# Reordering the last two experts of a one-core attention and mixture-of-experts layer: up, up, down, down, with the last down weights in smaller pieces and the output sent from two queues

## The chip, the cores and the metric

The kernel runs on one core of a Trainium2 chip. The metric is the device time of that core in microseconds (us). All matrices are fp32.

## What is computed

One layer over 256 tokens of 1024 features: an attention part with two kinds of heads, then a mixture of 32 experts, of which each token uses 4, and a final normalisation. The part that matters here, cut from the reference:

```
def clamped_swiglu(h):
    g = jnp.minimum(h[..., 0::2], SWIGLU_LIMIT)
    u = jnp.clip(h[..., 1::2], -SWIGLU_LIMIT, SWIGLU_LIMIT)
    return g * jax.nn.sigmoid(SWIGLU_ALPHA * g) * (u + 1.0)

def expert_block(args):                      # for every expert, on the tokens routed to it
    xb, e = args
    a = clamped_swiglu(xb @ w_up[e] + b_up[e])     # w_up[e]   1024 x 2048
    return a @ w_down[e] + b_down[e]               # w_down[e] 1024 x 1024
...
x = x + moe_ffn(...)                         # sum of the experts' rows times their router weights
return rmsnorm(x, final_norm_g)              # over the 1024 features
```

All 32 experts are computed, so all 32 pairs of weight matrices (12.6 MB each) pass from HBM to the core.

## The kernel before

**Weights.** An expert's weights are six units of 2 MB: four of `w_up` (u = 0 to 3) and two of `w_down` (u = 4 and 5). They pass through a ring of ten units in SBUF (`ring`), filled by DMAs that SyncE (SP) issues in order. Units are counted by g = 6 b + u, where b is the expert. A unit g is loaded once unit g-10 has been used (`used(g - UNITS)`; semaphores `up_used` and `down_used`). For the last expert, b = 31, unit u = 3 and unit u = 5 are loaded as two halves each (`load_half`, line 482), and the second half has a semaphore of its own, `last_half_in`.

**TensorE (PE).** The engine's instructions stand in the order in which the code writes them. For an expert b (`run`): `up_bias` (line 1109), `up` (line 1129: 16 fp32 matmul records for each unit), `gather(b+1)` (line 1084: tokens of the next expert), `combine(b-1)` (line 1174: adds the previous expert's rows times router weights to the four output banks 4 to 7), `combine_turn(b)` (line 1142), `gather_turn(b+1)` (line 1099), `act_turn(b)` (line 1148: transposes the activations), `down` (line 1162: 16 records for each unit). The result of `down` lies in PSUM bank `XG`.

**VectorE (DVE) and ScalarE (ACT).** `swiglu` (lines 1613, 1614, 1616, 1620) and ACT's `sigmoid` (line 811) turn the up product into activations. `act_turn` waits for them (`a_ready`). After it DVE (line 1648) and ACT (line 820) each copy half of the transposed activations `aT` to SBUF, which `down` waits for. ACT copies the combine weights `cT` (line 818) and, after `down`, its result `yv` (line 823), which `combine` waits for.

**The last expert before.** Its order on PE is `up`, `combine(30)`, `combine_turn(31)`, `act_turn(31)`, `down`, `combine(31)`. Its swiglu is written in two halves (`swiglu_last`, lines 1626 to 1644, and ACT lines 850 and 852): the first half starts when the first half of the up product's columns is complete (`half_up`).

**The end.** Each of the four output banks is squared and summed by ACT (`square_sum`, line 874) as `combine(31)` completes it. DVE adds the two sums of a token tile (`mean`, line 1349), ACT takes the root (`take_root`, line 663), and DVE inverts it (`invert`, line 1354). Tile 0 is scaled by DVE (line 1758) and ACT (line 888), tile 1 by DVE (`finish`, line 1762). SP issues the four output DMAs of 256 KB (lines 579 and 581).

Of the kernel before, what the change touches and what calls it, by code (L numbers as in the profile page):

```python
# [20 lines left out]
P = 128  # L21
# [13 lines left out]
EPS = 1e-5  # L35


def hybrid_layer(nc, x, attn_norm_g, w_in, cmp_pe_k, cmp_pe_v, cmp_w1_k, cmp_w2_k, cmp_w1_v, cmp_w2_v, w_out,
# [53 lines left out]
    with ctx:  # L92
# [118 lines left out]
        aT = xg.rearrange("p (a b) -> p a b", a=4)  # L211
        xgT = carve(512, 8, 64)
        dump = [xg, xgT.rearrange("p a b -> p (a b)")]
        cnt = carve(1)
# [41 lines left out]
        last_half_in = {u: sem(f"last_half_in{u}") for u in (3, 5)}  # L256
# [76 lines left out]
        half_up = sem("half_up")  # L333
        last_swi = sem("last_swi")
        last_sig = sem("last_sig")
# [9 lines left out]
        half_summed = sem("half_summed")  # L345
        scaled_by_g = sem("scaled_by_g")
# [47 lines left out]
        def job_bank(name):  # L394
            return ps[:, PJ[job_at[name] % 2], :]

# [36 lines left out]
        def _(sp):  # L433
# [126 lines left out]
            for g in range(EXPERT_UNITS * LATE, EXPERT_UNITS * E):  # L560
                b, u = g // EXPERT_UNITS, g % EXPERT_UNITS
# [90 lines left out]
        def _(act):  # L652
# [159 lines left out]

            def read_rest(b, prev):

                act.wait_ge(cT_done, b + 1)
                if prev:
                    act.wait_ge(comb_done, b)
                act.activation(cT, ps[:, XG, 0:256].rearrange("p (n q) -> p n q", n=2), ACT.Copy).then_inc(cT_read, 1)  # L818
                act.wait_ge(aT_done, b + 1)
                act.activation(aT[:, 0:2, :], UP[:, 0, 0:256].rearrange("p (a q) -> p a q", a=2), ACT.Copy)\  # L820
                   .then_inc(aT_read, 1)
                act.wait_ge(down_used, b * DOWN_UNITS + DOWN_UNITS)
                act.activation(yv, ps[:, XG, :], ACT.Copy).then_inc(y_read, 1)  # L823
# [53 lines left out]
            flat = work[:, 0:3 * 512].rearrange("p (a b) -> p a b", a=3)  # L877
            square_sum(0, 0, flat[:, 0, :])
            square_sum(0, 1, flat[:, 1, :])
            square_sum(1, 0, flat[:, 2, :])  # L880
            take_root(4)
            square_sum(1, 1, dump[1])
            take_root(5)
            act.wait_ge(rstd_ready, 5)
            for half in range(2):
                h = slice(512 * half, 512 * half + 512)
                act.wait_ge(scaled_by_g, half + 1)
                act.activation(xs[:, 0, h], xs[:, 0, h], ACT.Copy, scale=rstd[:, 4:5]).then_inc(fin_act, 1)


        @block.tensor
        def _(pe):
# [221 lines left out]
            def up(b, prev, unit, biased=False, last=False, halves=False):  # L1114
# [4 lines left out]
                for u in range(UP_UNITS):  # L1119
                    w = unit(u)  # L1120
                    for j in range(2):
                        k = 2 * u + j
                        if last and k == KD - 1:
                            pe.wait_ge(last_half_in[u], 16)
                        row = aside if halves and k == 1 else w[:, j * 2 * F:(j + 1) * 2 * F]
                        row = row.rearrange("k (p h x) -> k p h x", h=2, x=8)
                        for a in range(2):
# [4 lines left out]
                            if last and k == KD - 1 and a == 0:  # L1132
                                t.then_inc(half_up, 1)
# [4 lines left out]
            def combine_turn(b, ahead):  # L1138
                pe.wait_ge(pw_ready, b + 1)
                pe.wait_ge(xg_read, b + 1 + ahead)  # L1140
                for n in range(NT):
                    t = pe.transpose(ps[:, XG, n * P:(n + 1) * P], pw[:, n, :], ident[:, :])  # L1142
# [9 lines left out]
            def down(b, unit, last=False):  # L1152
# [3 lines left out]
                for u in range(DOWN_UNITS):  # L1156
                    w = unit(UP_UNITS + u)
                    for j in range(4):
                        if last and (u, j) == (1, 2):
                            pe.wait_ge(last_half_in[UP_UNITS + u], 16)  # L1160
                        for h in range(2):
                            t = pe.matmul(ps[h * 64:(h + 1) * 64, XG, :],  # L1162
                                          aT[:, j, u * 64:u * 64 + 64],
                                          w[:, j * D + h * 512:j * D + (h + 1) * 512],
                                          start=(u == 0 and j == 0), stop=(u == DOWN_UNITS - 1 and j == 3),
                                          skip_group_check=True)
                    t.then_inc(down_used, 1)

            def combine(b, first=False, last=False):

                pe.wait_ge(y_read, b + 1)
                for n in range(NT):
                    for h in range(2):
                        t = pe.matmul(ps[:, OUT[n][h], :], cT[h * 64:(h + 1) * 64, n, :], yv[h * 64:(h + 1) * 64, :],  # L1174
                                      start=first, stop=True, skip_group_check=True)
                        if last and (n, h) != (1, 1):
                            t.then_inc(half_summed, 1)
                t.then_inc(comb_done, 1)

# [8 lines left out]
            def in_singles(b):  # L1188

                def unit(u):  # L1190
                    pe.wait_ge(*single_in(EXPERT_UNITS * b + u))
                    return single(EXPERT_UNITS * b + u)
# [106 lines left out]
            for b in range(TAIL, E - 1):  # L1299
# [31 lines left out]
        def _(dve):  # L1331
# [290 lines left out]
            def swiglu_last(b):  # L1622

                lo, hi = slice(0, 64), slice(64, P)
                dve.wait_ge(half_up, 1)
                dve.tensor_scalar(t1[:, :, lo], up_pairs[:, 0][:, :, lo], 7.0, None, ALU.min).then_inc(last_swi, 1)
                dve.tensor_scalar(t3[:, :, lo], up_pairs[:, 1][:, :, lo], 7.0, -7.0, ALU.min, ALU.max)\
                   .then_inc(last_swi, 1)
                dve.wait_ge(last_swi, 2)
                dve.scalar_tensor_tensor(out=t3[:, :, lo], in0=t3[:, :, lo], scalar=1.0, in1=t1[:, :, lo],  # L1630
                                         op0=ALU.add, op1=ALU.mult).then_inc(last_swi, 1)
                dve.wait_ge(up_used, b * UP_UNITS + UP_UNITS)
                dve.tensor_scalar(t1[:, :, hi], up_pairs[:, 0][:, :, hi], 7.0, None, ALU.min).then_inc(swi, 1)
                dve.tensor_scalar(t3[:, :, hi], up_pairs[:, 1][:, :, hi], 7.0, -7.0, ALU.min, ALU.max).then_inc(swi, 1)
# [163 lines left out]
```

## Time and profile before

| what | value |
|---|---|
| runs of the kernel | 1081.4, 1081.66, 1081.82 us, median 1081.66 us |
| span of the profiled execution, first to last instruction | 1078.8 us |
| whole device time of the profiled execution | not given by itself; the median of the runs lies 2.9 us above the span |
| PE busy | 1028.3 us, 95% |
| mean transfer rate from HBM | 392 GB/s over the span |
| granted TensorE clock | 0.999 of full speed |

The span is what the rows below are measured in. The 2.9 us around it lie outside of every row.

### The profile page before, as it was taken

To read this page: it belongs to the slowest core of one execution; us is meant where nothing else is said; L and a number is where in the kernel's file an instruction comes from. 1 tells how busy PE (TensorE), PEld (TensorE's weight loads), DVE (VectorE), ACT (ScalarE), POOL (GpSimd) and SP (SyncE) were. 2 spreads that over 40 slices of the span, in tenths; PEclk is the share of its full clock that TensorE was granted. 3 is DMA by queue.
4 is the path that set the end of the run, shared out by engine and by line. 5 is a ranking of instruction groups with operands and counts; after the bars stand their busy time and mean duration, and the time that the engine had idled before them with its cause. 6 is when DMAs were issued, how large, how long until landed. Compare 5 with 4: busy or idle time off the path is not lost.

```text
span 1078.8 us, 12673 instructions
## 1 busy us (share of the span) xinstructions
PE 1028.3 (95%) x5097; PEld 409.9 (38%) x5097; DVE 223.3 (21%) x637; ACT 155.0 (14%) x388; POOL 20.6 (2%) x49
## 2 busy tenths in 40 slices
PE   7899999999999999999999999999999999999996
PEld 5686654333333333333333333333333333333332
DVE  3344433111111111111111111111112101111112
ACT  2323332011000011111111111111101100111102
POOL 4001000000000000000000000000000000000000
PEclk9999999999999999999999999999999999999999
DMA  9982469999999999999999999999999999999994
GB/s 281 315 313 93 157 252 378 399 405 426 429 426 433 433 431 430 432 431 432 430 433 429 435 431 433 431 429 435 431 431 431 430 433 424 428 427 427 428 426 201
DMA packets 36827, 423.34 MB, mean 392 GB/s; under 512 B 8226, under 2 KB 12370, under 8 KB 18996
## 3 DMA queue, kind: packets, MB, share of 16 engines
q1 hardware_dynamic: 36644, 422.37, 93.8%
q8 instruction: 31, 0.51, 0.2%
q10 hardware_dynamic: 144, 0.39, 0.1%
q14 instruction: 8, 0.07, 0.0%
HBM read 421.70 MB, written 1.05 MB: 392 GB/s over the span
## 4 chain that ended last, share of the span: by engine, by line
PE 77%; DMA 18%; DVE 3%; ACT 1%; issue 1%; DVEq 0%; SPq 0%
PE ps L1129 31%; DMA ring<-in_w_up_dram 18%; PE ps L1162 17%; PE ps L1174 5%; PE ps L1084 4%; PE ps L916 4%; PE ps L994 3%; PE ps L923 2%; PE ps L1109 2%; PE ps L945 1%; DVE work L1604 1%; PE ps L1099 1%; DVE work L1648 1%; PE ps L1142 1%; PE ps L1021 1%; PE ps L1033 1%
## 5 line engine op out<-in xcount | busy, mean ns | idle before, releaser
L1129 PE MATMUL ps<-ring,work 128*64 128x512 f32 x2040 | 447.2, 594 | 8.3 <-DMA ring<-in_w_up_dram 8.2
L1129 PEld LDWEIGHTS ps<-ring,work 128*64 128x64 f32 x2040 | 142.8, 137 | 309.7 <-issue 290.9
L1162 PE MATMUL ps<-ring,work 128*64 128x512 f32 x1008 | 223.3, 595 | 21.1 <-DVE work L1648 21.1
L1613 DVE TENSOR_SCALAR work<-ps 128x512 f32<-128x512 f32 x31 | 21.4, 691 | 641.4 <-PE ps L1129 641.4
L1162 PEld LDWEIGHTS ps<-ring,work 128*64 128x64 f32 x1008 | 69.8, 137 | 154.4 <-issue 129.0
L811 ACT ACTIVATE work<-work 128x512 f32<-128x512 f32 x31 | 19.5, 630 | 453.1 <-DVE work L1613 453.1
L1174 PE MATMUL ps<-work 64*128 64x512 f32 x256 | 63.6, 615 | 0.7 <-ACT work L823 0.7
L1084 PE MATMUL ps<-xt,work 128*64 128x512 f32 x256 | 60.6, 593 | 0.2 <-DVE work L1562 0.2
L823 ACT ACTIVATE work<-ps 128x512 f32<-128x512 f32 x32 | 19.1, 597 | 236.6 <-PE ps L1162 236.6
L916 PE MATMUL ps<-ring 128*128 128x256 f32 x192 | 42.5, 380 | 0.0
L916 PEld LDWEIGHTS ps<-ring 128*128 128x128 f32 x192 | 36.0, 190 | 5.0 <-issue 0.4
L1174 PEld LDWEIGHTS ps<-work 64*128 64x128 f32 x256 | 22.0, 186 | 41.8 <-issue 40.2
L1109 PE MATMUL ps<-work 32*64 32x512 f32 x256 | 34.8, 613 | 0.5 <-ACT work L846 0.5
L1604 DVE TENSOR_TENSOR work<-ps,gf_rowsT 128x512 f32<-128x512 f32 x32 | 22.1, 692 | 54.3 <-PE ps L1099 54.3
L1084 PEld LDWEIGHTS ps<-xt,work 128*64 128x64 f32 x256 | 18.2, 137 | 35.8 <-issue 35.4
L994 PE MATMUL ps<-ring,extra 128*128 128x512 f32 (+1 forms) x72 | 28.7, 546 | 0.0
L923 PE MATMUL ps<-ring 128*128 128x280 f32 (+1 forms) x64 | 21.9, 497 | 0.0
L1616 DVE SCALAR_TENSOR_TENSOR work<-work 128x512 f32<-128x512 f32 x31 | 21.5, 692 | 1.1
L1620 DVE TENSOR_TENSOR work<-work 128x512 f32<-128x512 f32 x31 | 21.4, 692 | 1.1
L1614 DVE TENSOR_SCALAR work<-ps 128x512 f32<-128x512 f32 x31 | 21.1, 680 | 0.0
L805 ACT ACTIVATE work<-ps 128x512 f32<-128x512 f32 x32 | 19.1, 597 | 11.2 <-PE ps L1084 11.2
L818 ACT ACTIVATE work<-ps 128x256 f32<-128x256 f32 x32 | 12.3, 385 | 51.0 <-PE ps L1142 51.0
(245 smaller groups left out, 521.3 us busy)
## 6 DMA issues: line engine op xcount, KB each, us to landing
ring<-in_w_up_dram SPq DMA_DIRECT2D x40, 4096.0 KB, 35.1
ring<-in_w_up_dram SPq DMA_DIRECT2D x44, 2048.0 KB, 16.6
ring<-in_w_down_dram SPq DMA_DIRECT2D x20, 4096.0 KB, 35.0
ring<-in_w_down_dram SPq DMA_DIRECT2D x21, 2048.0 KB, 14.8
ring<-in_w_in_dram SPq DMA_DIRECT2D x8, 1024.0 KB, 8.5
ring<-in_w_up_dram SPq DMA_DIRECT2D x7, 1024.0 KB, 12.0
ring<-in_w_out_dram SPq DMA_DIRECT2D x4, 1024.0 KB, 10.0
ring<-in_w_down_dram SPq DMA_DIRECT2D x4, 1024.0 KB, 29.1
```

The costliest lines, as they stand in the source:

```text
L916: t = pe.matmul(dst, lhs(win_unit(c, k)), xT[:, k, :], start=(k == 0), stop=(k == KD - 1))
L923: t = pe.matmul(dst, xT[:, k, n * P:(n + 1) * P], win_unit(c, k)[:, lo:hi], start=(k == 0), stop=(k == KD - 1))
L994: t = pe.matmul(dst, oT[:, k, n * P:(n + 1) * P], wout_nsa[:, k, lo:hi] if k < 4 else wout_moba[:, lo // 512, k % 4, lo % 512:lo % 512 + h ...
L1084: t = pe.matmul(ps[h * 64:(h + 1) * 64, XG, :], pm[:, n, :], xt[:, n, h * 512:(h + 1) * 512], start=(n == 0), stop=(n == 1), skip_group_ch ...
L1109: t = pe.matmul(UP[h * 64:h * 64 + 64, a, :], sel[a * E:a * E + E], bup[a * E:a * E + E, :].rearrange("e (p h x) -> e p h x", h=2, x=8)[:, ...
L1129: t = pe.matmul(UP[h * 64:h * 64 + 64, a, :], xgT[:, k, :], row[:, a * 64:(a + 1) * 64, h, :], start=False, stop=(k == KD - 1), skip_group ...
L1162: t = pe.matmul(ps[h * 64:(h + 1) * 64, XG, :], aT[:, j, u * 64:u * 64 + 64], w[:, j * D + h * 512:j * D + (h + 1) * 512], start=(u == 0 a ...
L1174: t = pe.matmul(ps[:, OUT[n][h], :], cT[h * 64:(h + 1) * 64, n, :], yv[h * 64:(h + 1) * 64, :], start=first, stop=True, skip_group_check=True)
L1604: dve.tensor_tensor(xgT.rearrange("p (h j) t -> p j h t", h=2), ps[:, XTB, :].rearrange("p (j h t) -> p j h t", j=4, h=2), gf_rowsT[:].uns ...
L1613: dve.tensor_scalar(t1, up_pairs[:, 0], 7.0, None, ALU.min).then_inc(swi, 1)
L1616: dve.scalar_tensor_tensor(out=t3, in0=t3, scalar=1.0, in1=t1, op0=ALU.add, op1=ALU.mult)\
L1620: dve.tensor_tensor(av, t3, t2, ALU.mult).then_inc(a_ready, 1)
```

## The change

The order of the last two experts becomes up(30), up(31), down(30), down(31), both in the loads (`turn_of` and `unit_of`) and on PE. The rows of down(31) go to PSUM bank `XTB`, and the transposed activations and combine weights of expert 31 to `aT_end` and `cT_end` (the places of `t1` and `t2`). `combine(30)` stands between the two units of down(31). Unit u = 3 of expert 31 is loaded in one piece, and its swiglu is the ordinary one. Unit u = 5 of expert 31 is loaded as one half and two quarters, with a semaphore each (`last_row_in`). In the final normalisation ACT takes the root from its own second sum, with the first sum (already divided and with the epsilon added, `end_base`) as the bias. ACT issues the output DMAs of tile 0 itself. The diff, cut to its core:

```diff
+        aT_end = t1
+        cT_end = t2[:, 0:2, :]
...
+        def turn_of(b, u):
+
+            if b < E - 2:
+                return EXPERT_UNITS * b + u
+            if u < UP_UNITS:
+                return EXPERT_UNITS * (E - 2) + UP_UNITS * (b - (E - 2)) + u
+            return EXPERT_UNITS * (E - 2) + 2 * UP_UNITS + DOWN_UNITS * (b - (E - 2)) + u - UP_UNITS
+
+        unit_of = {turn_of(b, u): (b, u) for b in range(E) for u in range(EXPERT_UNITS)}
...
-                b, u = g // EXPERT_UNITS, g % EXPERT_UNITS
+                b, u = unit_of[g]
                 used(g - UNITS)
-                if b == E - 1 and u in last_half_in:
+                if (b, u) == (E - 1, EXPERT_UNITS - 1):
                     load_half(b, u, 0, half_of(single(g), 0), place_in[spot(g - 1)])
-                    load_half(b, u, 1, half_of(single(g), 1), last_half_in[u])
+                    for i in range(2):
+                        sp.dma_start(single(g)[:, (2 + i) * D:(3 + i) * D], down_v[b][:, (6 + i) * D:(7 + i) * D])\
+                          .then_inc(last_row_in[i], 16)
...
-                sp.wait_ge(fin_act, half + 1)
-                sp.dma_start(out_v[0][:, h], xs[:, 0, h]).then_inc(out_sent, 16)
                 sp.wait_ge(fin_dve, half + 1)
                 sp.dma_start(out_v[1][:, h], xs[:, 1, h]).then_inc(out_sent, 16)
...
-            with act.Fori(TAIL, E - 1) as i:
+            with act.Fori(TAIL, E - 2) as i:
                 run(i)
-            act.wait_ge(last_swi, 1)
-            act.activation(t2[:, :, 0:64], t1[:, :, 0:64], ACT.Sigmoid, scale=1.702).then_inc(last_sig, 1)
-            act.wait_ge(swi, (E - 1) * 3 + 1)
-            act.activation(t2[:, :, 64:P], t1[:, :, 64:P], ACT.Sigmoid, scale=1.702).then_inc(sig_done, 1)
+            select(E - 1, E - 1)
+            sigmoid(E - 2)
+            read_xg(E - 1)
+            act.wait_ge(comb_done, E - 2)
+            read_cT(E - 2, cT, XG)
+            read_aT(E - 2, aT)
+            sigmoid(E - 1)
             act.activation(root[:, 5:6], ident[:, 0:1], ACT.Sqrt)
-            read_rest(E - 1, True)
+            read_aT(E - 1, aT_end)
+            read_cT(E - 1, cT_end, XTB)
+            read_y(E - 2)
+            act.wait_ge(down_used, E * DOWN_UNITS)
+            act.wait_ge(comb_done, E - 1)
+            act.activation(yv, ps[:, XTB, :], ACT.Copy).then_inc(y_read, 1)
...
+            def end_root(n):
+                act.wait_ge(squared[0], 8 + 2 * n)
+                act.wait_ge(base_ready, n + 1)
+                act.activation(root[:, 4 + n:5 + n], sq_sum[:, 4 + n, 1:2], ACT.Sqrt, scale=1.0 / D, bias=ms[:, 4 + n:5 + n])\
+                   .then_inc(rooted, 1)
...
                 act.activation(xs[:, 0, h], xs[:, 0, h], ACT.Copy, scale=rstd[:, 4:5]).then_inc(fin_act, 1)
+                act.wait_ge(fin_act, half + 1)
+                act.dma_start(out_v[0][:, h], xs[:, 0, h]).then_inc(out_sent, 16)
...
-            last = in_singles(E - 1)
-            up(E - 1, True, last, last=True)
+            unit, last = in_singles(E - 2), in_singles(E - 1)
+            up(E - 2, True, unit)
+            gather(E - 1)
+            combine(E - 3)
+            combine_turn(E - 2, 1)
+            gather_turn(E - 1)
+            act_turn(E - 2)
+            up(E - 1, True, last)
+            act_turn(E - 1)
+            combine_turn(E - 1, 0, XTB)
+            down(E - 2, unit)
+            pe.wait_ge(aT_read, E * 2)
+            pe.wait_ge(cT_read, E)
+            down_unit(E - 1, 0, last(UP_UNITS), aT_end, XTB)
             combine(E - 2)
-            combine_turn(E - 1, 0)
-            act_turn(E - 1)
-            down(E - 1, last, last=True)
-            combine(E - 1, last=True)
+            down_unit(E - 1, 1, last(UP_UNITS + 1), aT_end, XTB, last=True)
+            combine_end(E - 1)
...
-            swiglu_last(E - 1)
-            read_aT(E - 1)
+            swiglu(E - 1)
+            read_aT(E - 1, aT_end)
...
             dve.wait_ge(gfin_in, 16)
+            end_base(0)
             scale_by_g(0)
-            mean(4, ((0, 8),))
             scale_by_g(1)
+            end_base(1)
             invert(4)
-            mean(5, ((0, 10),))
             invert(5)
```

`down_unit` is the body of the old `down` for one unit, with the place of the activations and the bank as arguments; with `last=True` it waits for `last_row_in` before each of its two last quarters. `combine_end` is `combine` with `cT_end`, and counts each output bank as the old last `combine` did.

## Rows read from the trace of the kernel before

**Rows 1.** Stretch 1040 to 1060 us, by windows: busy per engine, clock, DMA share, GB/s.

```profile
1040.00:1060.00 20.00, 19.68 (x95) 6.00 (x92) 2.66 (x8) 2.14 (x4) 0.00 (x0) 1.00 1.00 421
```

**Rows 2.** PE's waits over the span: total us, times, longest.

```profile
PE ps L1129 <- DMA ring<-in_w_up_dram: 8.2, 9, 1.4
```

**Rows 3.** Timeline of PE, 1026 to 1072 us: start, us, instructions, idle before.

```profile
1026.35 3.65 PE L1129 MATMUL ps<-ring,work 128*64 128x512 f32 x16 [1.24 <-DMA ring<-in_w_up_dram]
...
1033.85 0.60 PE L1099 MATMUL ps<-ident,work 128*128 128x128 f32 x4
1034.28 0.60 PE L1148 MATMUL ps<-ident,work 128*128 128x128 f32 x4
...
1035.56 7.09 PE L1162 MATMUL ps<-ring,work 128*64 128x512 f32 x32 [0.68 <-DVE work L1648]
...
1042.58 1.09 PE L1109 MATMUL ps<-work 32*64 32x512 f32 x8
...
1043.60 7.09 PE L1129 MATMUL ps<-ring,work 128*64 128x512 f32 x32
...
1051.00 7.09 PE L1129 MATMUL ps<-ring,work 128*64 128x512 f32 x32 [0.32 <-DMA ring<-in_w_up_dram]
...
1058.02 1.99 PE L1174 MATMUL ps<-work 64*128 64x512 f32 x8
...
1060.34 0.66 PE L1148 MATMUL ps<-ident,work 128*128 128x128 f32 x4
...
1061.51 7.09 PE L1162 MATMUL ps<-ring,work 128*64 128x512 f32 x32 [0.52 <-DVE work L1648]
...
1069.30 1.99 PE L1174 MATMUL ps<-work 64*128 64x512 f32 x8 [0.70 <-ACT work L823]
```

**Rows 4.** Timeline of DVE, swiglu and aT copy of expert 30.

```profile
1030.05 0.69 DVE L1613 TENSOR_SCALAR work<-ps 128x512 f32<-128x512 f32 x1 [23.06 <-PE ps L1129]
...
1032.10 0.69 DVE L1620 TENSOR_TENSOR work<-work 128x512 f32<-128x512 f32 x1
...
1035.09 0.41 DVE L1648 COPY work<-ps 128x256 f32<-128x256 f32 x1
```

**Rows 5.** Last weight loads: PE's wait for the tenth, then two issues with landings.

```profile
1055.97 0.37 PEld L1129 LDWEIGHTS ps<-ring,work 128*64 128x64 f32 x4 [0.48 <-DMA ring<-in_w_up_dram]
...
L472 SPq DMA_DIRECT2D ring<-in_w_down_dram x1: 4357/4357/4357, 1017.7 to 1017.7; - x1
DMA to landing us min/median/max: 43.1/43.1/43.1
...
L482 SPq DMA_DIRECT2D ring<-in_w_down_dram x2: 4240/4241/4242, 1022.1 to 1026.4; - x2
DMA to landing us min/median/max: 39.4/40.3/41.2
```

**Rows 6.** The end of the timeline, and ACT's two early DMA issues.

```profile
1073.16 0.15 DVE L1349 TENSOR_REDUCE ms<-sq_sum 128x1 f32<-128x2 f32 x1 [0.48 <-ACT work L874]
1073.35 0.29 ACT L663 ACTIVATE root<-ms,eps 128x1 f32<-128x1 f32 x1 [0.29 <-DVE ms L1349]
...
1073.88 1.41 DVE L1762 SCALAR_TENSOR_TENSOR extra<-ps,rstd,extra 128x512 f32<-128x512 f32 x2
...
1075.66 0.45 SPq L581 DMA_DIRECT2D out_dram<-extra  x1
...
L749 ACTq DMA_DIRECT2D work<-in_b_up_dram x2: 389/414/439, 80.3 to 80.7; - x2
```

**Rows 7.** PE's first instruction, and clock and DMA of two stretches.

```profile
6.90 1.94 PE L898 MATMUL ps<-ident,extra 128*128 128x128 f32 x8 [6.90 <-ACT extra L669]
...
3.00:6.00 3.00, 0.00 (x0) 0.00 (x0) 1.79 (x9) 1.22 (x4) 2.76 (x4) 1.00 1.01 338
...
1075.50:1076.00 0.50, 0.00 (x0) 0.00 (x0) 0.00 (x0) 0.00 (x0) 0.00 (x0) 0.74 1.01 373
```

More of the change, by code:

```diff
@@ L255, in hybrid_layer @@
         pair_in = [sem(f"pair_in{u}") for u in range(PAIRS)]
-        last_half_in = {u: sem(f"last_half_in{u}") for u in (3, 5)}
+        last_row_in = [sem(f"last_row_in{i}") for i in range(2)]
         prm_in = sem("prm_in")
@@ L345, in hybrid_layer @@
         half_summed = sem("half_summed")
+        base_ready = sem("base_ready")
         scaled_by_g = sem("scaled_by_g")
@@ L1112, in up_bias, with up @@
                 t.then_inc(bias_used, 1)
-            def up(b, prev, unit, biased=False, last=False, halves=False):
+            def up(b, prev, unit, biased=False, halves=False):
                 if not biased:
@@ L1122, in up @@
                         k = 2 * u + j
-                        if last and k == KD - 1:
-                            pe.wait_ge(last_half_in[u], 16)
                         row = aside if halves and k == 1 else w[:, j * 2 * F:(j + 1) * 2 * F]
@@ L1136, in up, with combine_turn @@
                     t.then_inc(up_used, 1)
-            def combine_turn(b, ahead):
+            def combine_turn(b, ahead, bank=XG):
                 pe.wait_ge(pw_ready, b + 1)
@@ L1150, in act_turn, with down_unit, down @@
                 t.then_inc(aT_done, 1)
-            def down(b, unit, last=False):
+            def down_unit(b, u, w, acts, bank, last=False):
+                for j in range(4):
+                    if last and j >= 2:
+                        pe.wait_ge(last_row_in[j - 2], 16)
+                    for h in range(2):
+                        t = pe.matmul(ps[h * 64:(h + 1) * 64, bank, :],
+                                      acts[:, j, u * 64:u * 64 + 64],
+                                      w[:, j * D + h * 512:j * D + (h + 1) * 512],
+                                      start=(u == 0 and j == 0), stop=(u == DOWN_UNITS - 1 and j == 3),
+                                      skip_group_check=True)
+                t.then_inc(down_used, 1)
+            def down(b, unit):
                 pe.wait_ge(aT_read, b * 2 + 2)
@@ L1156, in down, with combine @@
                 for u in range(DOWN_UNITS):
[L1157 to L1169, printed above, removed]
+                    down_unit(b, u, unit(UP_UNITS + u), aT, XG)
+            def combine(b, first=False, weights=cT):
                 pe.wait_ge(y_read, b + 1)
@@ L1173, in combine, with combine_end @@
                     for h in range(2):
-                        t = pe.matmul(ps[:, OUT[n][h], :], cT[h * 64:(h + 1) * 64, n, :], yv[h * 64:(h + 1) * 64, :],
+                        t = pe.matmul(ps[:, OUT[n][h], :], weights[h * 64:(h + 1) * 64, n, :], yv[h * 64:(h + 1) * 64, :],
                                       start=first, stop=True, skip_group_check=True)
-                        if last and (n, h) != (1, 1):
-                            t.then_inc(half_summed, 1)
                 t.then_inc(comb_done, 1)
+            def combine_end(b):
+                pe.wait_ge(y_read, b + 1)
+                for n in range(NT):
+                    for h in range(2):
+                        pe.matmul(ps[:, OUT[n][h], :], cT_end[h * 64:(h + 1) * 64, n, :], yv[h * 64:(h + 1) * 64, :],
+                                  start=False, stop=True, skip_group_check=True)\
+                          .then_inc(half_summed if (n, h) != (1, 1) else comb_done, 1)
             def in_pairs(m, c):
@@ L1190, in unit @@
                 def unit(u):
-                    pe.wait_ge(*single_in(EXPERT_UNITS * b + u))
-                    return single(EXPERT_UNITS * b + u)
+                    pe.wait_ge(*single_in(turn_of(b, u)))
+                    return single(turn_of(b, u))
                 return unit
@@ L1298, in _ @@
                     run(m * CYCLE + (SINGLES + r), in_pairs(m, r))
-            for b in range(TAIL, E - 1):
+            for b in range(TAIL, E - 2):
                 table_read = tables(b)
@@ L1753, in total, with end_base @@
                 return ps[:, OUT[n][half], :]
+            def end_base(n):
+                dve.wait_ge(squared[0], 7 + 2 * n)
+                dve.tensor_scalar(ms[:, 4 + n:5 + n], sq_sum[:, 4 + n, 0:1], 1.0 / D, EPS, ALU.mult, ALU.add)\
+                   .then_inc(base_ready, 1)
             def scale_by_g(half):
```

67 lines of the change are left out of this document (23 added, 44 removed).

## The prediction

> **What bounds the kernel now.** I read four views, from the whole to the end. The windows come first: between 1040 and 1060 us PE is busy 19.68 of 20 us and the DMA engines are full at 421 GB/s [rows 1]. So in the expert stage both resources are nearly exhausted together. Second, the waits: PE waited for weights only nine times, 8.2 us in all [rows 2]. The stream of weights is the slower of the two, by a little. Third, PE's timeline over the last two experts [rows 3] with the landings of the last loads [rows 5]. The reader is to see where the stream stops deciding. Call the last twelve units of the stream the 1st to the 12th. The 9th lets PE go on at 1051.00 [rows 3], the second half of the 10th at 1055.97, the 11th lands at 1017.7 + 43.1 = 1060.8, and the two halves of the 12th at 1022.1 + 41.2 = 1063.3 and 1026.4 + 39.4 = 1065.8 [rows 5]. That is 4.9 us for a unit, while PE needs 3.44 us for one (7.09 for x32 less 3.65 for x16 [rows 3]). From 1051 on PE never waits for weights again except for that half: down(31) runs without a break from 1061.51 to 1068.60 [rows 3], and its last quarter, due at some 1067.7, had landed 2 us before. Fourth, the end of the timeline [rows 6]: after 1068.60 comes a chain of copies, sums, root, scaling and output.
>
> So the question is not when the last weights land but what PE still has to do, and what it waits for, from the point where the new order departs from the old.
>
> **The new order step by step.** The first new instruction on PE stands after `act_turn(30)`, where `down(30)` used to start at 1035.56, released by DVE's copy of `aT` (1035.09 + 0.41 [rows 4]). `up_bias(31)` waits for the same copy, so it starts at 1035.56 too. No load is gated differently: the last twelve loads wait for units of experts 28 and 29 and the first two of expert 30, whose use does not move, and all units are equally large. I therefore keep the landings by place in the stream.
>
> - Bias: 1042.58 to 1043.60, thus 1.02 us [rows 3]; up(31) starts at 1036.58.
> - up(31): 3.65 + 3 x 3.44 = 13.97 us, to 1050.55. Its units are now the 5th to 8th; the 8th lands about 4.9 us before the 9th, near 1046.1, and is wanted at 1036.58 + 3 x 3.44 = 1046.9. No wait for weights.
> - swiglu(31) lies bare. `act_turn(31)` is next on PE and waits for it, and queued behind it are `combine_turn(31)` and all of `down(30)`, whose activations have been ready since 1035.5. The ordinary swiglu takes 0.05 + 2.74 us (1030.05 to 1032.10 + 0.69 [rows 4], after the up product ended at 1030.00 [rows 3]), and PE starts 0.05 later: 1053.39. PE idles 2.8 us. Before, `combine(30)` (1.99 us) and the two-half swiglu covered this: PE went from 1058.02 to 1060.34 without idling [rows 3].
> - Six transposes at 0.43 us for four (1033.85 to 1034.28 [rows 3]), 0.65 us, and 0.14 for the change of shape (7.02 between starts against 6.88 for two units [rows 3]): down(30) starts at 1054.2. The copies of `aT` and `cT` of expert 31 are hidden behind it; before, PE idled 0.52 us for them [rows 3].
> - down(30): 6.88 us to 1061.08. It wants the 9th unit at 1054.2 and the 10th at 1057.6; both are there.
> - First unit of down(31): the 11th, landed at 1060.8, 0.3 us before it is wanted; to 1064.52. This is the thinnest margin.
> - `combine(30)`: 0.14 for the shape and 1.9 us; its copy `yv` was made behind the unit before. To 1066.56.
> - Second unit of down(31): 3.65 us, to 1070.2. Its last quarter is wanted near 1069.1 and landed at 1065.8. The split into quarters is therefore worth nothing here; its cover is 3.3 us.
>
> PE's last down matmul ends at 1070.2 against 1068.60: **1.6 us later**. In sum, 2.8 us of bare swiglu and its hand-over are paid, and what comes back is the two small stalls (0.32 for weights, 0.52 for the copies [rows 3]) and a few tenths of shape changes. The bounds of this step are 1.2 (transposes and shape changes free) and 2.2 us (the 11th unit some tenths late, each shape change at 0.2).
>
> **The end.** Copying `yv` and `combine(31)` keep their durations. The root no longer passes through DVE's sum: 1073.16 to 1073.35 [rows 6] goes, 0.2 us. `end_base(0)`, 0.15 us, is added on DVE ahead of `scale_by_g(0)`, in time that DVE spends waiting. Output: `finish` ends at 1073.88 + 1.41 = 1075.29, but SP issues the last transfer at 1075.66, since it issues four at 0.45 us each [rows 6]. With two on each queue the last issue of SP can follow at once, 0.3 to 0.35 us earlier. On ACT a scaling of 0.66 us, an issue of about 0.41 us [rows 6] and the second scaling lead to an issue at about the same moment. The transfers themselves take all DMA engines, 373 GB/s at a share of 1.01 [rows 7], so the 1 MB needs about 2.8 us whoever issues it; that caps the gain. I take 0.35 us, bounds 0 and 0.6. The Trainium skill says the same in DMA: Bandwidth & Descriptors, section Issuing engines are not separate DMA queues: starting transfers from several engines saves only the time to initiate them. By that rule alone the gain would be the 0.37 us between `finish` and the last issue; the trace agrees with its full share.
>
> Sum: +1.6 - 0.2 - 0.35 = +1.05 us, with bounds +0.4 (1.2 - 0.2 - 0.6) and +2.0 (2.2 - 0.2 - 0). The span goes from 1078.8 to 1079.85 and, with the 2.9 us around it unchanged, the median from 1081.66 to 1082.7. A difference under 0.2% (2.2 us) cannot be told from none in a measurement of this kernel, so this counts as no change.
>
> **Rival 1: the stream of weights decides the end (faster).** If PE had nothing left to do but the last quarter once it lands, the down product would end at 1065.8 + 0.86 + 0.21 = 1066.9, 1.7 us before 1068.60, and with the 0.55 us of the end the kernel would take 1079.4 us, 0.21% less. For it: the stream is full until 1060 [rows 1], and PE did wait for the 9th and the half of the 10th. Against it: by my steps PE is 3.3 us behind the stream at the end. It decides only if the bare swiglu costs nothing and another half microsecond goes. Partly true (a swiglu half covered) it gives 1081.3, which is no change.
>
> **Rival 2: TensorE's clock falls in the new gap (slower).** PE idles 2.8 us right after a dense stretch. After the last matmul (1069.30 + 1.99 = 1071.29 [rows 3]) the granted clock still stood at full until the stretch 1075.5 to 1076.0, whose mean of 0.74 puts the fall from 2.4 to 1.2 GHz at about 1075.8 [rows 7]. That fall came after 4.5 us of idling. In the first 6.9 us, PE idle, the row from 3 to 6 us shows 1.00 [rows 7]. Both speak against a fall after 2.8 us, but where a fall falls cannot be settled by two cases. Price: at half the clock a down unit takes 3.44 us more, so one unit at the lower level gives 1086.1 us; it tells from 1.2 us of loss on. The Trainium skill (TensorE: Matmul & The Clock Gate, section Why this matters for your kernels) warns against leaving TensorE idle between bursts of matmuls, since the clock then drops to half; by it the change would be slower, while the rows show no fall in an idle stretch as short as this one.
>
> **Rival 3: the reorder starves PE earlier.** If the 8th or 11th unit lands a microsecond later than its place says, PE waits for it and the end shifts by as much: 1083.7. The 0.3 us of margin at the 11th is all that stands against it. It stays within no change, barely.
>
> **How the numbers follow.** My forecast (+0.4 to +2.0) 0.72; rival 3, 0.08; rival 1 in full 0.03 and in part 0.06; rival 2, 0.11. The likeliest time is 1082.7, its own range 1082.1 to 1083.7. Widened to the partial rival 1 on one side and to rival 3 with a short low clock on the other, the range is 1081.4 to 1083.9. Faster by over 0.2% (below 1079.5): 0.04. Slower (above 1083.8): 0.13. Within: 0.83.
>
> **What the changed profile would show.** PE's `up_bias(31)` at 1035.6; a single idle stretch of about 2.8 us before `act_turn(31)` near 1053.4, ended by DVE's last swiglu operation; down(30) from 1054.2 with no wait for weights; the last down matmul ending near 1070.2; landings unchanged at 1060.8 and 1065.8; clock 1.00 from 1053 to 1070; one operation fewer between the last square and the root; the last output issue within 0.1 us after `finish`. The prediction is wrong if PE waits for weights in the down stage, if the gap before `act_turn(31)` is much shorter than 2.8 us, or if the clock drops.

## The result and the profile after

The changed kernel took 1083.24 us in the median of 16 runs (1081.66 to 1086.58), the kernel before 1081.53 us in 16 runs beside it (1080.47 to 1082.6). The ratio is 1.0022, 95% interval 1.0015 to 1.0029: slower by 0.2%, some 2.4 us by the ratio (the means, 1083.8 and 1081.5 us, lie 2.3 apart) and 1.7 us by the medians. The time lies inside the forecast range, but the interval lies wholly above 1, where the forecast was no change, and the runs spread over 4.9 us where those of the kernel before spread over 2.1.

The profiled execution of the changed kernel took 1082.32 us, with a span of 1080.1 us. Its timeline of PE, which answers to [rows 3]:

```profile
1035.51 1.09 PE L1144 MATMUL ps<-work 32*64 32x512 f32 x8 [0.77 <-DVE work L1675]
1036.53 13.95 PE L1162 MATMUL ps<-ring,work 128*64 128x512 f32 x64
1053.32 0.65 PE L1179 MATMUL ps<-ident,work 128*128 128x128 f32 x4 [2.84 <-DVE work L1671]
1053.81 0.38 PE L1173 MATMUL ps<-ident,work 128*128 128x128 f32 x2
1054.12 10.52 PE L1189 MATMUL ps<-ring,work 128*64 128x512 f32 x48
1064.58 1.99 PE L1208 MATMUL ps<-work 64*128 64x512 f32 x8
1066.49 3.65 PE L1189 MATMUL ps<-ring,work 128*64 128x512 f32 x16
1070.85 1.99 PE L1217 MATMUL ps<-work 64*128 64x512 f32 x8 [0.70 <-ACT work L882]
```

The x64 group is up(31), all four units in one piece: no weights are waited for. Then PE idles 2.84 us for the last operation of swiglu(31) (DVE line 1671). The x48 group is down(30) and the first unit of down(31), again without a wait for weights. The last down matmul ends at 1066.49 + 3.65 = 1070.14, against 1061.51 + 7.09 = 1068.60 before [rows 3]: 1.54 us later.

The end on all engines, which answers to [rows 6]:

```profile
1074.64 0.29 ACT L908 ACTIVATE root<-sq_sum,ms 128x1 f32<-128x1 f32 x1
1074.84 0.70 ACT L921 ACTIVATE extra<-extra,rstd 128x512 f32<-128x512 f32 x1
...
1075.23 1.41 DVE L1794 SCALAR_TENSOR_TENSOR extra<-ps,rstd,extra 128x512 f32<-128x512 f32 x2
1075.58 0.38 ACTq L923 DMA_DIRECT2D out_dram<-extra  x1
1076.01 0.72 ACT L921 ACTIVATE extra<-extra,rstd 128x512 f32<-128x512 f32 x1 [0.46 <-ACT extra L921]
1076.76 0.37 ACTq L923 DMA_DIRECT2D out_dram<-extra  x1
...
1076.01 1.00 SPq L592 DMA_DIRECT2D out_dram<-extra  x2
```

From the last down matmul to the first operation of DVE's `finish` it is 5.09 us (1070.14 to 1075.23) against 5.28 before (1068.60 to 1073.88 [rows 6]): the shorter root gives its 0.19 us. From the end of `finish` to the end of the span it is 1080.1 - 1076.64 = 3.46 us against 1078.8 - 1075.29 = 3.51: the second queue gives 0.05 us. The last issue (ACT, 1076.76) now stands 0.12 us behind the end of `finish` instead of 0.37. The first issue (ACT, 1075.58) stands 4.5 us before the end of the span, as it did before (SP, 1074.28, also 4.5 us).

So this one execution is 1.3 us longer in its span, and every step on PE stands where the forecast had put it. Its clock, by windows (the same columns as [rows 1]), is full behind the gap:

```profile
1052.00:1054.00 2.00, 0.68 (x6) 0.64 (x6) 1.23 (x2) 1.39 (x2) 0.00 (x0) 1.00 1.02 434
1054.00:1056.00 2.00, 2.00 (x12) 0.73 (x12) 0.42 (x1) 0.66 (x2) 0.00 (x0) 1.00 0.94 397
```

What it does not explain is the spread up to 1086.6. Over all executions of the changed kernel in this study (16 here, 11 and 8 as controls below), 15 of 35 took 1084 us or more; of the 73 executions of the kernel before that ran beside the experiments none took more than 1082.97. The mean granted clock of each execution is known. The 14 with 0.998 have a median of 1082.4 us and none is above 1083.3; the 8 with 0.992 or less are all at 1084.85 or above. The 13 between them are mixed, from 1082.2 to 1086.3 us.

### The profile page after: what moved, and what is told of

Same layout as the page of the kernel before. It is cut to its first block, busy times and chain, and to the rows that moved or that the text cites. A ratio compares the mean times of both kernels' runs of the same rounds, so it can differ in the third digit from the quotient of the medians.

```text
span 1080.1 us, 12662 instructions
## 1 busy us (share of the span) xinstructions
PE 1030.6 (95%) x5097; PEld 410.9 (38%) x5097; DVE 222.9 (21%) x633; ACT 154.9 (14%) x387; POOL 20.7 (2%) x49
## 3 DMA queue, kind: packets, MB, share of 16 engines
HBM read 421.70 MB, written 1.05 MB: 391 GB/s over the span
## 4 chain that ended last, share of the span: by engine, by line
PE 84%; DMA 11%; DVE 3%; ACT 1%; issue 1%; DVEq 0%; ACTq 0%; SPq 0%
PE ps L1162 36%; PE ps L1189 19%; DMA ring<-in_w_up_dram 10%; PE ps L1208 5%; PE ps L1119 4%; PE ps L951 4%; PE ps L1029 3%; PE ps L1144 2%; PE ps L958 2%; PE ps L980 1%; DVE work L1655 1%; PE ps L1134 1%; DVE work L1675 1%; PE ps L1173 1%; PE ps L1056 1%
## 5 line engine op out<-in xcount | busy, mean ns | idle before, releaser
L1179 PE MATMUL ps<-ident,work 128*128 128x128 f32 x128 | 19.3, 273 | 2.8 <-DVE work L1671 2.8
```

## The experiments

**Theory A**: the new order costs about 1 us always, and in some executions TensorE's clock also falls in the 2.84 us gap. **Theory B**: the loss is an even one and the clock has no part in it.

**e0_again and e9_again2: the changed kernel, unaltered**, as controls.

> The changed kernel itself, as the control of this group. Theory A (the new order costs about 1 us always, and in some executions TensorE's clock falls in the 2.8 us gap before act_turn(31), which costs some 3.4 us more): the runs fall into two groups, about 1082.5 us and about 1085.5 us, with a mean clock near 0.998 or 0.995 in the first and 0.995 or 0.992 in the second. Theory B (the loss is an even one of 1.7 to 2.4 us, the clock has no part in it): one group around 1083.2 us, whatever the mean clock.

Measured: 1083.3 us (1081.89 to 1085.27, 11 runs), ratio 1.0017 (1.0008 to 1.0026). Its profiled execution, 1084.85 us with a span of 1082.6, shows what the first profile did not. PE's timeline, then the windows:

```profile
1036.57 1.09 PE L1144 MATMUL ps<-work 32*64 32x512 f32 x8 [0.77 <-DVE work L1675]
...
1054.39 1.11 PE L1179 MATMUL ps<-ident,work 128*128 128x128 f32 x4 [2.85 <-DVE work L1671]
1055.29 0.63 PE L1173 MATMUL ps<-ident,work 128*128 128x128 f32 x2
1055.86 11.27 PE L1189 MATMUL ps<-ring,work 128*64 128x512 f32 x48
...
1068.98 3.65 PE L1189 MATMUL ps<-ring,work 128*64 128x512 f32 x16
```

```profile
1052.00:1054.00 2.00, 0.00 (x0) 0.00 (x0) 1.93 (x4) 1.67 (x2) 0.00 (x0) 1.00 1.00 426
1054.00:1056.00 2.00, 1.61 (x8) 1.28 (x10) 0.76 (x2) 0.87 (x4) 0.00 (x0) 0.50 1.04 442
1056.00:1058.00 2.00, 2.00 (x8) 0.58 (x10) 0.00 (x0) 0.35 (x1) 0.00 (x0) 0.65 0.99 418
```

The granted clock, third number from the end of a row, is 0.50 from 1054 us on, that is 1.2 instead of 2.4 GHz, while PE stands idle, and is back at full from about 1057.4 on. The four transposes take 1.11 us instead of 0.65 and the x48 group 11.27 instead of 10.52. From the start of `up_bias(31)` to the end of the last down matmul it is 36.06 us (1036.57 to 1072.63), against 34.63 us (1035.51 to 1070.14) in the first profile: the fall costs 1.43 us.

> The changed kernel once more, as the control of this group. By the reading so far: about 1082.3 us where no clock fall adds anything, 1085 and more where the clock falls in the gap, in about a third of the runs; median 1083.2.

Measured: 1084.02 us (1081.76 to 1086.34, 8 runs), ratio 1.0025 (1.0014 to 1.0036). Four runs lie at 1081.8 to 1083.0, four at 1085.0 to 1086.3, and none between. The profiled execution again has a fall, now just after PE had taken up work: the two windows, then the same x48 group of PE's timeline.

```profile
1054.00:1056.00 2.00, 1.24 (x8) 0.83 (x10) 1.12 (x2) 1.37 (x4) 0.00 (x0) 0.93 1.00 422
1056.00:1058.00 2.00, 2.00 (x6) 0.49 (x4) 0.00 (x0) 0.11 (x1) 0.00 (x0) 0.50 1.00 422
```

```profile
1036.94 1.09 PE L1144 MATMUL ps<-work 32*64 32x512 f32 x8 [0.77 <-DVE work L1675]
...
1054.76 0.66 PE L1179 MATMUL ps<-ident,work 128*128 128x128 f32 x4 [2.84 <-DVE work L1671]
...
1055.56 12.22 PE L1189 MATMUL ps<-ring,work 128*64 128x512 f32 x48
...
1069.63 3.65 PE L1189 MATMUL ps<-ring,work 128*64 128x512 f32 x16
```

Here the six transposes run at full clock, and the fall hits the first down unit only: 12.22 us against 10.52. The whole stretch takes 36.34 us (1036.94 to 1073.28), 1.71 us more than without a fall. Both profiles also show that `up_bias(31)` starts 1.1 and 1.4 us later than in the first profile. That part of their extra time arises before the changed code, and the traces show where. In e0_again the clock also fell at about 40.3 us, in the attention part, for 3.4 us. The first profile's window and e0_again's:

```profile
40.00:45.00 5.00, 4.91 (x45) 3.30 (x47) 3.15 (x17) 2.61 (x10) 0.00 (x0) 1.00 1.13 335
```

```profile
40.00:45.00 5.00, 5.00 (x32) 2.99 (x34) 2.46 (x12) 2.54 (x10) 0.00 (x0) 0.66 1.13 312
```

The 64 matmul records from there on took 8.81 us instead of 7.13, and `up_bias(0)` started 1.0 us later (169.70 instead of 168.71). In e9_again2 the clock is full there and `up_bias(0)` is on time (168.68). Its delay comes between 638 and 676 us, where the wait for `w_up` ends 1.4 us later than in the first profile (675.58 instead of 674.16).

**e2_long: the gap doubled.** DVE does the first operation of swiglu(31) four more times, to no use:

```diff
+            dve.wait_ge(up_used, E * UP_UNITS)
+            for _ in range(4):
+                link(dve.tensor_scalar(t1, up_pairs[:, 0], 7.0, None, ALU.min))
             swiglu(E - 1)
```

> The changed kernel with the gap before act_turn(31) doubled: DVE repeats the first operation of swiglu(31) four times, 0.6 to 0.75 us each, so PE idles some 5.6 us instead of 2.84. Theory A: the clock falls in every execution in or right behind the gap, the profile shows it, and the time rises by 2.8 us for the wait and by some 3.4 us for the clock: about 1088.5 to 1089 us in all runs, with little spread. Theory B: the wait alone, 1086 us against 1083.2 of the control.

Measured: 1088.41 us (1088.02 to 1088.89, 5 runs), ratio 1.0066 (1.0052 to 1.0079), all within 0.9 us. In the one profile the gap is 5.75 us, and the clock is low from 2.1 us into it (1053.9) until PE has worked again for some 3 us (1060.7):

```profile
1057.57 1.11 PE L1179 MATMUL ps<-ident,work 128*128 128x128 f32 x4 [5.75 <-DVE work L1671]
...
1059.04 11.35 PE L1189 MATMUL ps<-ring,work 128*64 128x512 f32 x48
```

```profile
1054.00:1056.00 2.00, 0.00 (x0) 0.00 (x0) 1.93 (x4) 0.51 (x1) 0.00 (x0) 0.50 0.99 422
...
1060.00:1062.00 2.00, 2.00 (x10) 0.61 (x8) 0.00 (x0) 0.00 (x0) 0.00 (x0) 0.81 0.79 324
```

The stretch from `up_bias(31)` to the last down matmul takes 39.04 us, 4.41 more than the 34.63 without a fall: 2.91 for the longer wait and 1.5 for the clock. The time of all runs is that of theory A and 2.4 us above theory B's 1086, but the sum behind it was another: it had 3.4 us for the clock where the trace has 1.5. This profile too has the fall at 40 us (0.66 from 40 to 45 us), and its `up_bias(31)` starts 1.3 us late (1036.85). So the hit in the median was in part luck; the fall in the gap is what the trace shows.

**e1_fill and e7_fill_pairs: matmuls in the gap.** Their results are not used. The first wrote only one half of the bank's partitions, the second wrote both halves in turn, as `up` does. This is the edit of the second:

```diff
             up(E - 1, True, last)
+            for _ in range(3):
+                for h in range(2):
+                    pe.matmul(ps[h * 64:h * 64 + 64, XTB, :], xgT[:, 0, :], xt[:, 0, 0:512],
+                              start=True, stop=True, skip_group_check=True)
             act_turn(E - 1)
```

> The changed kernel with six matmuls of 512 columns, whose result nobody reads, put into the gap on PE between up(31) and act_turn(31). They take about 6 x 0.43 = 2.6 us, less than the 2.84 us of the gap, so no other instruction moves. Theory A: the clock never falls there; every run at 1082 to 1083 us, the upper group of the control is missing. Theory B: as the control, also in its highest runs. The end of the down product stays at 1070.1 us from the start of the span in both.

Measured: 1086.51 us (1085.7 to 1087.54, 5 runs). This filler missed its purpose: its 12 records took 5.3 us, not 2.6, so in the profile `act_turn(31)` came 2.2 us later behind the start of up(31) (19.03 us instead of 16.79). It says nothing on the clock except that the profile shows no fall in this place. It has the one at 40 us.

> The filler of e1_fill took 5.24 us instead of 2.6, since its matmuls all wrote the same 64 rows of PSUM; this one writes the two halves in turn as up does, six matmuls in 12 records at 0.215 us, thus 2.6 us inside the 2.84 us gap. Theory A (the clock falls in the gap in some executions and costs some 2.5 us in them): all runs in the lower group, 1081.7 to 1083.5 us, median 1082.4, none above 1084. Theory B (the upper group has another cause): 4 of 10 runs above 1084, as in the 27 runs of the changed kernel so far.

Measured: 1084.03 us (1083.18 to 1084.99, 10 runs), ratio 1.0024 (1.0014 to 1.0033). The filler fits, and the clock is full from 1040 us to the last matmul:

```profile
1052.35 2.75 PE L1357 MATMUL ps<-xt,work 128*64 128x512 f32 x12
1055.36 0.65 PE L1179 MATMUL ps<-ident,work 128*128 128x128 f32 x4 [0.27 <-DVE work L1675]
...
1056.16 10.52 PE L1189 MATMUL ps<-ring,work 128*64 128x512 f32 x48
```

The stretch takes 34.63 us (1037.55 to 1072.18), to the hundredth that of the changed kernel without a fall. The spread shrinks from the controls' 3.4 and 4.6 us to 1.8, but the median is 1.6 us above the expected 1082.4. From the last down matmul to the end of the span this profile has 10.7 us instead of 10.0 (1072.18 to 1082.9; 1070.14 to 1080.1): the output transfers land 3.1 and 3.2 us after their issue instead of 2.3 and 2.5, and a second load of instructions falls into the same stretch. The control's end (e0_again, 10.0 us) had one such load; e1_fill's end, with two, is 10.6 us long. That accounts for 0.7 us in this profile. Its `up_bias(31)` also starts 2.0 us late (1037.55), of which 1.1 us stand there from the first expert on (`up_bias(0)` at 169.83), behind a fall of the clock at 40 us (0.66 from 40 to 45 us). Whether that holds for the median is not shown.

By its times this run does not favour theory A. Five of ten runs are above 1084 us, where A had none and B had four. With 0.7 us taken off for the longer end two are left, the higher at 1084.3, and the control's runs at 1085 and above have no counterpart. But the median is then 1083.3, that of e0_again, and not 1082.4. The filler removes the fall from the trace and the highest times, and it does not show that the fall raises the median.

**e3_cover: the gap filled with useful work.** The first unit of down(30) moves ahead of `act_turn(31)` (`down_unit` has no wait for `aT` and `cT` of its own, so PE gets the two waits):

```diff
             up(E - 1, True, last)
+            pe.wait_ge(aT_read, (E - 1) * 2)
+            pe.wait_ge(cT_read, E - 1)
+            down_unit(E - 2, 0, unit(UP_UNITS), aT, XG)
             act_turn(E - 1)
             combine_turn(E - 1, 0, XTB)
-            down(E - 2, unit)
+            down_unit(E - 2, 1, unit(UP_UNITS + 1), aT, XG)
```

> The changed kernel with the first unit of down(30) put before act_turn(31) on PE, so that it covers swiglu(31). Theory A with the stream as the next limit: down(30) starts at 1050.95 us when the 9th unit lands, its second unit waits until the 10th is there at 1055.95, down(31) until the 11th at 1060.8, and the down product ends at 1070.0, no earlier than in the changed kernel; but no idle stretch is above 1.5 us, so the clock never falls and all runs are at 1082 to 1083 us. A rival (the prediction's reading, that the bare swiglu is what is paid): the 2.8 us come back, and the kernel takes 1080 us or less in the lower group.

Measured: 1082.84 us (1081.73 to 1083.72, 11 runs), ratio to the kernel before 1.0012 (1.0003 to 1.0021). The 2.8 us do not come back, since weights are now waited for:

```profile
1037.28 1.09 PE L1144 MATMUL ps<-work 32*64 32x512 f32 x8 [0.77 <-DVE work L1678]
...
1052.54 3.65 PE L1189 MATMUL ps<-ring,work 128*64 128x512 f32 x16 [0.29 <-DMA ring<-in_w_down_dram]
...
1057.34 3.65 PE L1189 MATMUL ps<-ring,work 128*64 128x512 f32 x16 [0.34 <-DMA ring<-in_w_down_dram]
1062.33 3.65 PE L1189 MATMUL ps<-ring,work 128*64 128x512 f32 x16 [1.33 <-DMA ring<-in_w_down_dram]
...
1067.83 3.65 PE L1189 MATMUL ps<-ring,work 128*64 128x512 f32 x16
```

The stretch takes 34.20 us (1037.28 to 1071.48) instead of 34.63. No idle stretch is above 1.4 us, the profile has no fall there, and none of the 11 runs reaches 1084. The profiled execution does have the fall at 40 us (0.66) and a late start, and still took no more than 1083.72 us.

**e4_combine_first: `combine(30)` ahead of down(31), on top of e3_cover.**

```diff
-            down_unit(E - 1, 0, last(UP_UNITS), aT_end, XTB)
             combine(E - 2)
+            down_unit(E - 1, 0, last(UP_UNITS), aT_end, XTB)
```

> e3_cover with combine(30) moved ahead of the first unit of down(31), where PE otherwise waits 1.3 us for the 11th unit. Theory (after the gap is covered, the stream of weights is the limit up to the 11th unit, and what stands behind it is paid in full): combine(30) then lies mostly in the wait and the down product ends 0.6 to 0.8 us earlier than in e3_cover, 33.5 us after the start of up_bias(31) instead of 34.2; median 1082.2. If combine(30) costs the same wherever it stands: 34.2 us again and 1082.8.

Measured: 1082.11 us (1080.92 to 1083.44, 11 runs), ratio 1.0007 (0.9998 to 1.0016). The stretch takes 33.53 us (1036.50 to 1070.03), 0.67 us less than in e3_cover, as expected: two thirds of a microsecond of combine(30) now lie in the wait for the 11th unit, and the change had put it behind that wait. Here too no run reaches 1084.

**e6_best and e10_best_again: all covers at once.** The order is up(31), both units of down(30), `act_turn(31)`, `combine_turn(31)`, `combine(30)`, down(31); the 10th unit is loaded in halves, and ACT copies `yv` first:

```diff
+                elif (b, u) == (E - 2, EXPERT_UNITS - 1):
+                    load_half(b, u, 0, half_of(single(g), 0), place_in[spot(g - 1)])
+                    load_half(b, u, 1, half_of(single(g), 1), mid_half_in)
...
             up(E - 1, True, last)
+            pe.wait_ge(aT_read, (E - 1) * 2)
+            pe.wait_ge(cT_read, E - 1)
+            down_unit(E - 2, 0, unit(UP_UNITS), aT, XG)
+            down_unit(E - 2, 1, unit(UP_UNITS + 1), aT, XG, mid=True)
             act_turn(E - 1)
             combine_turn(E - 1, 0, XTB)
-            down(E - 2, unit)
+            combine(E - 2)
             pe.wait_ge(aT_read, E * 2)
             pe.wait_ge(cT_read, E)
             down_unit(E - 1, 0, last(UP_UNITS), aT_end, XTB)
-            combine(E - 2)
```

> The changed kernel with PE ordered up(31), down(30), act_turn(31), combine_turn(31), combine(30), down(31), and the 10th unit loaded in two halves. swiglu(31) is covered by down(30), the copy of yv by the transposes, the wait for the 11th unit by combine(30). By the stream's landings the down product ends about 32.4 us after the start of up_bias(31), against 34.6 in the changed kernel and 33.1 in the kernel before, and with the new end the kernel is at 1080.6 to 1081.0 us with no upper group. If the clock or the stream has another limit: no better than the kernel before, 1081.6 us or more.

Measured: 1080.63 us (1079.63 to 1083.15, 11 runs), ratio 0.9996 (0.9987 to 1.0005).

```profile
1035.94 1.09 PE L1148 MATMUL ps<-work 32*64 32x512 f32 x8 [0.77 <-DVE work L1684]
...
1051.20 7.09 PE L1195 MATMUL ps<-ring,work 128*64 128x512 f32 x32 [0.29 <-DMA ring<-in_w_down_dram]
...
1061.09 7.09 PE L1195 MATMUL ps<-ring,work 128*64 128x512 f32 x32
```

The stretch takes 32.24 us (1035.94 to 1068.18), 2.4 less than in the changed kernel and 0.8 less than the 33.04 of the kernel before (1035.56 to 1068.60 [rows 3]).

> The kernel of e6_best again, beside the changed kernel and the kernel before on one chip. Theory: 2 to 2.7 us faster than the changed kernel in the median, and 0.5 us faster than the kernel before, which 11 runs did not settle (0.9996, 0.9987 to 1.0005). Rival: level with the kernel before.

Measured: 1080.69 us (1080.15 to 1081.59, 11 runs) beside 1084.02 of the changed kernel and 1081.21 of the kernel before; ratio to the latter again 0.9996 (0.9987 to 1.0005). Of the changed kernel's 8 runs none is as fast as its slowest. Against the kernel before both medians are 0.5 us lower, but both intervals hold 1, so that this order is faster than the kernel before is not shown.

**e5_end_only: the new end alone, on the kernel before** (the `end_base`, `end_root` and ACT-queue edits of the diff, nothing else).

> The kernel before with only the new end: the root taken from ACT's own second sum, and tile 0 sent from ACT's queue. From the two profiles the end (last down matmul to end of span) is 0.25 us shorter in the changed kernel, against 0.55 predicted. So 1081.3 us against 1081.55, which a measurement of this kernel hardly tells, and never more than 0.6 us faster. If the new end is to blame for a part of the loss: above 1081.6 us.

Measured: 1081.53 us (1080.18 to 1082.82, 11 runs), ratio 1.0004 (0.9995 to 1.0013). The new end is worth nothing that shows in the times: the median beside it was 1081.18, so the expected gain was missed, within the interval. In the profile the end, from the last down matmul to the end of the span, is 9.9 us (1068.88 to 1078.8) against 10.2 before, the 0.3 us that the changed kernel shows too.

**e8_whole: the last unit in one piece** (PE's waits for the quarters go as well).

```diff
-                    load_half(b, u, 0, half_of(single(g), 0), place_in[spot(g - 1)])
-                    for i in range(2):
-                        sp.dma_start(single(g)[:, (2 + i) * D:(3 + i) * D], down_v[b][:, (6 + i) * D:(7 + i) * D])\
-                          .then_inc(last_row_in[i], 16)
+                    load_unit(b, u, single(g), place_in[spot(g - 1)])
```

> The changed kernel with the last down unit loaded in one piece. Prediction's reading: its pieces land by 1065.8 us and the unit is wanted from 1066.5 us on, so the split is worth nothing; median and spread as the control, the down product's end 34.6 us after the start of up_bias(31). Rival (the quarters pay): PE waits ahead of the last unit and the control is faster by up to 1 us.

Measured: 1082.34 us (1082.06 to 1086.45, 7 runs), ratio 1.0027 (1.0014 to 1.0039), against 1.0025 of the control. The profile has the same stretch, 34.64 us (1035.16 to 1069.80), and no fall. The pieces are worth nothing in this order. The two groups of times are there again: four runs at 1082.1 to 1082.3, three at 1084.7 to 1086.5.

## Why the prediction was right and where it failed

- **The steps on PE held.** Bias at 1035.51 (forecast 1035.56), up(31) without a wait, 2.84 us of idling (2.8), down(30) from 1054.12 (1054.2), no wait for the 11th unit, the end at 1070.14 (1070.2). The 1.6 us were 1.54. Rival 3 did not come: no profile of the changed kernel shows a wait for weights there.
- **The root held**, 0.19 of 0.2 us. **The second queue was mis-sized**: 0.35 us forecast, 0.05 measured. The term took the time from the end of `finish` to the last issue as gain. But the transfers keep all DMA engines full once the first has begun [rows 7], and the span ended 4.5 us after the first issue in both kernels, so an earlier last issue moved nothing. With it the sum is +1.3 us, which is the difference of the two spans. The bound of 0 had been in the forecast.
- **The step that failed is the rejection of rival 2**, that the rows show no fall in an idle stretch as short as this one, and with it a sum that has no term for the clock. It rested on one fall 4.5 us after the last matmul and on the first 6.9 us. The clock does fall there in some executions: two of four profiles of this order (both controls; not the first profile and not e8_whole) have it, at 1054.0 and 1055.8, that is 2.5 and 3.8 us after the last up matmul, and in the profile of the doubled gap it comes 2.1 us after it. The Trainium skill's warning against idle gaps between bursts (TensorE: Matmul & The Clock Gate, section Why this matters for your kernels) was the better guide than the two rows that were set against it. The two traces with a fall agree with it, although the page's warning is for gaps a little longer than these 2.84 us; two traces of the same gap show none. The fall was treated as an alternative to the forecast, when it comes on top of it in a part of the executions and so belongs in the sum. As an estimate: 1.3 us always, and 1.4 to 1.7 us in 15 of 35 executions, if each run of 1084 us or more has a fall there, give a mean of 1.9 to 2.0 us out of the measured 2.3. That each has one is not shown.
- **Its price was mis-sized too**: 3.44 us forecast, 1.43, 1.71 and 1.5 us in three traces. The price took the clock as low for a whole down unit at half speed, 6.9 us. In both falls in the short gap it was low for about 3.4 us (1054.0 to 1057.4, 1055.8 to 1059.2), and in the first of them 0.4 us of that was idle time.
- **The call of no change had a second fault.** It held that 0.2% cannot be told from none. The interval of 16 runs against 16 is 0.07% to either side, so the sum of +1.05 us (0.10%) and the +1.3 us of the two spans (0.12%) would both have shown as slower, without any fall.
- **The 2.9 us around the span** were the median of some runs less the span of another execution. Wherever an execution has both numbers on record the difference is 2.0 to 2.3 us, so the profiled execution before took about 1081.0 us (an estimate), less than the median. That the measured 1083.24 lies within the range is in part luck too: it is the middle of two groups of runs, near 1082.4 and near 1085.3 us, and the upper one lies outside.
- **What the bare swiglu costs** was right for this order and wrong as a reason. Covering it gave back 0.43 of 2.84 us (e3_cover), since the stream then holds PE three times. Of the rest, 0.7 us lie in the place of combine(30) (e4_combine_first), and 1.3 us in what e6_best changes on top of it: `act_turn(31)` behind both units of down(30), the 10th unit in halves and `yv` copied first. These three were not separated.

**What stays open.** The upper runs of the changed kernel lie some 2.9 us above the lower ones (medians 1085.3 at a clock of 0.992 or less, 1082.4 at 0.998), of which the two traces put 1.4 and 1.7 us into the gap. The rest goes with a start of `up_bias(31)` that is 1.1 and 1.4 us later: once behind a fall at 40 us, once behind a longer wait for weights, both ahead of the changed code. For theory A speaks that with the gap covered no run reaches 1084 (0 of 22 in e3_cover and e4_combine_first, whose stretches are only 0.4 and 1.1 us shorter, against 15 of 35); against it as the whole cause, the median of e7_fill_pairs. The fall at 40 us is in five profiles (e0_again, e1_fill, e2_long, e3_cover, e7_fill_pairs) of the eleven with the new order on PE and in neither of the two with the old one, which is too few to say that the change has no part in it. Lower mean clocks occur in the kernel before as well, where the 21 runs with 0.993 or 0.994 lie about 1 us above the 17 with 0.999 (medians near 1081.8 and 1080.8). Late starts also occur without a fall in the gap (e3_cover 1037.28, e7_fill_pairs 1037.55). Why in the changed kernel both profiles with a late start have a fall there too was not settled, nor is a mean clock enough to say of a single run where it fell.

## What to carry to other kernels

The time that this reorder costs on PE came out of the timeline to a tenth of a microsecond, but each new idle stretch on TensorE of some microseconds needs a second term, the clock, with a share of the executions in which it is paid. Ask of a stall not only how long it is but what would hold the engine if it were gone: here most of 2.84 us would have been waiting for weights. When the transfers at the end run at full rate, as here, ask for the first issue and not for the last. And before a small difference is called no change, compare it with the interval that the number of runs will give.

## What the runs showed of the hardware

**The clock also falls without idling.** In the profile of the changed kernel PE is busy from 805 to 825 us, and the clock is low for about 6.9 of them:

```profile
805.00:810.00 5.00, 5.00 (x26) 1.58 (x22) 0.00 (x0) 0.00 (x0) 0.00 (x0) 1.00 0.99 426
810.00:815.00 5.00, 5.00 (x14) 1.68 (x10) 1.64 (x9) 0.60 (x1) 0.00 (x0) 0.81 1.00 433
815.00:820.00 5.00, 5.00 (x17) 1.31 (x18) 0.00 (x0) 0.26 (x1) 0.00 (x0) 0.50 0.99 426
820.00:825.00 5.00, 5.00 (x26) 1.57 (x24) 0.00 (x0) 0.00 (x0) 0.00 (x0) 1.00 1.03 446
```

What PE did before it fell, at about 813.1 us, were matmuls over 32 rows (`down_bias`, from 810.55 us). The kernel before has the same matmuls there, and its profile shows no fall. The same happens in e5_end_only, whose PE order is that of the kernel before. It puts PE back by 3.4 us against the profile of the kernel before (the next `gather` starts at 832.27 instead of 828.88). PE's slack to the stream of weights takes it up again: `up_bias(30)` is 1.7 us late (1014.65 instead of 1012.97), and what follows `act_turn(30)` starts at 1035.51 instead of 1035.56.

**It falls behind short idle stretches too.** Ahead of the fall at 40.3 us in e0_again PE idled for 1.59 us, did three transposes, idled for 0.43 us and did three more. The first profile has the same idle stretches there and no fall.

**Matmuls that all write the same 64 output partitions took twice as long.** In e1_fill 12 records took 5.31 us; the same 12 with the two halves in turn took 2.75 us (e7_fill_pairs).

**A few more instructions can cost at another place.** With both fillers the end is 0.6 to 0.7 us longer, with no change to its code, and both profiles show a second instruction load beside the output transfers, where the others show one. That the load is the cause is argued, not shown.
